# Reciprocal row sums inside the probability transposes: a diagonal in place of the identity, the sink as a score column, transposes two pairs behind the scores

## The reference

```python
# layer 0: the sink is one more logit, whose probability is dropped
p = jax.nn.softmax(jnp.concatenate([s_loc, s_ctx, sink_l], axis=-1), axis=-1)
o = (jnp.einsum('bhgnqk,bhnkd->bhgnqd', p[..., :nk].astype(v.dtype), vb)
     + jnp.einsum('bhgnql,bhld->bhgnqd', p[..., nk:nk + L].astype(v.dtype), vc))
...
# layer 1: no sink
p = jax.nn.softmax(jnp.concatenate([s_loc, s_ctx], axis=-1), axis=-1)
```

## Time and profile before

| | us |
|---|---|
| median of 3 runs | 1751.51 (1749.96 to 1753.03) |
| profiled execution, its own time | 1752.69 |
| its span in the trace | 1750.9 |
| TensorE busy | 1667.4 (95%) |
| VectorE, ScalarE, GpSimd busy | 708.4, 644.1, 676.9 |
| attention of layer 0 | about 269 to 358 |
| attention of layer 1, with the context values | about 1194 to 1315 |
| granted TensorE clock over the span | 0.99 |

### The profile page before, as it was taken

One profiled execution on the slowest core, in us unless ns is written; L12 is line 12 of the kernel. 1 busy time (PEld: TensorE's weight loads), 2 busy tenths in 40 slices (PEclk: granted clock), 3 DMA queues, 4 the chain that ended last, 5 costly groups with the idle time before them and its releaser, 6 DMA issues.

```text
span 1750.9 us, 25757 instructions
## 1 busy us (share of the span) xinstructions
PE 1667.4 (95%) x10178; PEld 1387.9 (79%) x10178; DVE 708.4 (40%) x1121; ACT 644.1 (37%) x1120; POOL 676.9 (39%) x456
## 2 busy tenths in 40 slices
PE   5999998999999999999899999999999899999997
PEld 2868886777877888878899878877887788888886
DVE  3335456717588735402555420005771551011103
ACT  4242215727422122213555343235772522222222
POOL 2212222038554544443542043334443444444443
PEclk9999999999999999999999999999999899999999
DMA  8643111023466746533556645433002353333331
GB/s 325 212 150 99 42 25 49 2 73 108 145 193 193 230 143 188 167 91 109 145 169 183 193 117 113 92 94 101 2 2 60 100 165 95 105 90 98 96 98 69
DMA packets 210131, 207.17 MB, mean 118 GB/s; under 512 B 16454, under 2 KB 180828, under 8 KB 209756
## 3 DMA queue, kind: packets, MB, share of 16 engines
q1 hardware_dynamic: 197352, 165.53, 31.7%
q10 hardware_dynamic: 12660, 39.99, 7.4%
HBM read 203.37 MB, written 2.13 MB: 117 GB/s over the span
## 4 chain that ended last, share of the span: by engine, by line
PE 82%; DVE 5%; issue 4%; POOL 3%; ACT 3%; DMA 2%; SPq 0%; ACTq 0%; POOLq 0%; DVEq 0%
PE ps L1689 39%; PE ps L1716 29%; PE ps L1867 3%; PE ps L1923 3%; PE ps L1888 3%; POOL w_lo L518 3%; DMA mod_early<-in_w_mod 1%; ACT w_hi L830 1%; PE ps L1763 1%; PE ps L1802 1%; DVE xs L1278 1%; PE ps L1935 1%; PE ps L2051 1%; DVE full L1227 1%; DMA w_raw<-in_w_ffn_in 1%
## 5 line engine op out<-in xcount | busy, mean ns | idle before, releaser
L518 POOL TENSOR_TENSOR w_lo<-w_raw,w_hi 128x1024 fp32r<-128x1024 f32 (+1 forms) x223 | 557.5, 2502 | 896.3 <-ACT w_hi L830 896.1
L1689 PE MATMUL ps<-h_hi,w_hi 128*128 128x512 f32 (+1 forms) x1488 | 496.7, 352 | 11.7 <-POOL w_lo L518 8.0
L1689 PE MATMUL ps<-h_hi,w_lo 128*128 128x512 f32 (+1 forms) x1488 | 492.0, 349 | 0.0
L1689 PE MATMUL ps<-h_lo,w_hi 128*128 128x512 f32 (+1 forms) x1488 | 491.0, 348 | 0.0
L830 ACT ACTIVATE w_hi<-w_raw 128x1024 fp32r<-128x1024 f32 (+1 forms) x275 | 287.2, 1046 | 354.2 <-PE ps L1716 342.8
L1689 PEld LDWEIGHTS ps<-h_hi,w_hi 128*128 128x128 f32 x1488 | 270.0, 189 | 56.6 <-issue 20.2
L1689 PEld LDWEIGHTS ps<-h_hi,w_lo 128*128 128x128 f32 x1488 | 269.8, 189 | 36.2
L1689 PEld LDWEIGHTS ps<-h_lo,w_hi 128*128 128x128 f32 x1488 | 269.8, 189 | 36.0
L518 DVE TENSOR_TENSOR w_lo<-w_raw,w_hi 128x1024 fp32r<-128x1024 f32 x52 | 69.2, 1332 | 200.5 <-ACT w_hi L830 197.5
L1716 PE MATMUL ps<-w_hi,hid_hi 128*128 128x512 f32 x440 | 136.7, 392 | 8.0 <-ACT mod_row L842 4.2
L1297 DVE TENSOR_TENSOR hid_f<-silu_g,ps 128x512 f32<-128x512 f32 (+1 forms) x66 | 39.3, 595 | 255.3 <-PE ps L1689 254.9
(11 more groups left out here) (213 smaller groups left out, 1790.4 us busy)
## 6 DMA issues: line engine op xcount, KB each, us to landing
w_raw<-in_w_ffn_in SPq DMA_DIRECT2D x132, 512.0 KB, 3.8
w_raw<-in_w_ffn_out SPq DMA_DIRECT2D x66, 512.0 KB, 3.5
mod_raw<-in_w_mod ACTq DMA_DIRECT2D x42, 512.0 KB, 4.5
w_raw<-in_na_w_in SPq DMA_DIRECT2D x32, 512.0 KB, 3.7
mod_early<-in_w_mod SPq DMA_DIRECT2D x30, 512.0 KB, 9.0
full<-in_w_mod ACTq DMA_DIRECT2D x15, 512.0 KB, 4.9
w_raw<-in_ab_w_in SPq DMA_DIRECT2D x9, 512.0 KB, 4.6
w_raw<-in_ab_w_in SPq DMA_DIRECT2D x16, 256.0 KB, 3.8
```

The lines of the kernel that those rows point to most:

```text
L518: eng.tensor_tensor(w_lo[:, u % RING, 0:width], w_raw[:, u % RAW, 0:width], w_hi[:, u % RING, 0:width].bitcast(F32), ALU.subtract).then_in ...
L1689: mm = pe.matmul(o[0], sta(x, o), mov(y, o), start=first and n == 0, stop=last and n == 2)
```

## The change

Every probability block is now multiplied by a diagonal matrix, where it was transposed by the identity: `pe.matmul` of the block against a 128x128 diagonal of the pair's reciprocal row sums. The transposed block comes out normalized. So the steps `shift`, `inverse`, `norms`, `inverse_rows` and `normalize` go, and `high` and `low` read the output's PSUM bank directly. The sink becomes column 0 of the score block in layer 0 (`prob0` has 1 + 5*128 columns), so that the row sum includes it. GpSimd writes that column (`sink_column`) and makes the two diagonals (`scale`): a power -1 of the two row sums, and a product of the identity with the result, 128x256, into one buffer, `full[:, 0:2]` in layer 0 and `scale1` in layer 1. `prob` has three buffers instead of two. Transposes stand two pairs behind the scores, values three. The third buffer of layer 1 lies where `gate_b` is, so ScalarE's load of the third gate rows moves behind attention of layer 1.

```diff
+            feed(sp("out0L") + 1)
+            def sink_column(p):
+                f = PAIRS[0][p][2]
+                if p >= 3:
+                    pool.wait_ge(at_p, 2 * (p - 2))
+                pool.tensor_scalar(prob0[:, p % 3, :, 0:1].rearrange("p x n -> p (x n)"), sink[:, f:f + 5:4], 1.0 / SCALE,
+                                   None, ALU.mult).then_inc(at_sink, 1)
+            def scale(layer, p):
+                q = PAIR0[layer] + p
+                n = CHUNK0[layer] + p // 2
+                pool.wait_ge(at_p, 2 * (q + 1))
+                if p:
+                    pool.wait_ge(at_ta, q)
+                    pool.wait_ge(at_tb, q)
+                    if fifths(layer, p - 1):
+                        pool.wait_ge(at_t5, fifths(layer, p - 1))
+                rows, inv = (x[:, 2 * (p % 2):2 * (p % 2) + 2] for x in (rowsum[:, n % 2, :], sm[:, n % 2, 3, :]))
+                pool.tensor_tensor(inv, rows, one_hot[:, 34:36], ALU.pow).then_inc(at_rinv, 1)
+                pool.wait_ge(at_rinv, q + 1)
+                one = ident[:]
+                one = bass.AP(one.tensor, one.offset, [list(one.ap[0]), [0, 2], [1, P]])
+                pool.tensor_tensor(scale_of(layer), one, bcast(inv, P), ALU.mult).then_inc(at_scale, 1)
+            for p in range(3):
+                sink_column(p)
+            for p in range(len(PAIRS[0])):
+                scale(0, p)
+                if p + 3 < len(PAIRS[0]):
+                    sink_column(p + 3)
             feed(sp("out0C"))
...
                     pool.wait_ge(v_mixed, p + 1)
+                if p:
+                    scale(1, p - 1)
+            scale(1, len(PAIRS[1]) - 1)
             feed(sp("out1L") + 7)
...
                 def softmax(p):
-                    n, c = s_cols(layer, p), c0 + p // 2
+                    n, c = s_cols(layer, p) + (layer == 0), c0 + p // 2
                     act.wait_ge(at_m, q0 + p + 1)
+                    if layer == 0:
+                        act.wait_ge(at_sink, p + 1)
...
-                for p in range(n_pairs + 3):
-                    if 1 <= p <= n_pairs:
-                        evacuate(p - 1)
-                    if p % 2 == 0 and p >= 4:
-                        inverse_rows(p // 2 - 2)
+                for p in range(n_pairs + 4):
+                    if p % 2 == 1 and p >= 5:
+                        high((p - 5) // 2)
+                    if 2 <= p <= n_pairs + 1:
+                        evacuate(p - 2)
                     if p < n_pairs:
                         softmax(p)
...
-                    if i == 6:
-                        gate_load(act, 2)
...
             attention(1, lambda: layer1_values("v1C", C_TILES))
+            act.wait_ge(at_p, 2 * (PAIR0[1] + len(PAIRS[1])))
+            act.wait_ge(at_ta, PAIR0[1] + len(PAIRS[1]))
+            act.wait_ge(at_tb, PAIR0[1] + len(PAIRS[1]))
+            gate_load(act, 2)
             feed(sp("out1L") + 7)
...
-                    if p >= 2:
-                        dve.wait_ge(at_ta, q0 + p - 1)
-                        dve.wait_ge(at_tb, q0 + p - 1)
+                    if p >= 3:
+                        dve.wait_ge(at_ta, q0 + p - 2)
+                        dve.wait_ge(at_tb, q0 + p - 2)
...
                 def turns(p):
                     n = s_cols(layer, p) // P
+                    pe.wait_ge(at_scale, q0 + p + 1)
                     for x in range(2):
-                        pe.wait_ge(at_p, 2 * (q0 + p) + x + 1)
                         claim(4 + x)
                         for j in range(min(n, 4)):
-                            mm = pe.transpose(ps(4 + x, j * P, (j + 1) * P), probs(p, x, j), ident[:])
+                            mm = pe.matmul(ps(4 + x, j * P, (j + 1) * P), probs(p, x, j), scale_of(layer)[:, x, :],
+                                           start=True, stop=True)
...
-                for p in range(n_pairs + 2):
+                for p in range(n_pairs + 3):
                     if p == 0:
                         start(lambda: scores(0))
                     elif p < n_pairs:
                         scores(p)
-                    if 1 <= p <= n_pairs:
-                        turns(p - 1)
-                    if p >= 2:
-                        values(p - 2)
-                        if p % 2 == 1:
-                            norms(p // 2 - 1)
+                    if 2 <= p <= n_pairs + 1:
+                        turns(p - 2)
+                    if p >= 3:
+                        values(p - 3)
```

More of the change, by code:

```diff
@@ L624, in scores_bank, with prob_of, scale_of @@
             return 2 * x if layer == 0 else 2 * x + p % 2
-        def mixed_out(layer):
-            return full[:, 0:2, :].rearrange("p k n -> p (k n)") if layer == 0 else on1[:]
+        def prob_of(layer, p, x):
+            if layer == 0:
+                return prob0[:, p % 3, x]
+            return prob1_c[:, x] if p % 3 == 2 else prob1[:, p % 3, x]
+        def scale_of(layer):
+            return full[:, 0:2, :] if layer == 0 else scale1[:]
         block = ctx.enter_context(nc.Block())
@@ L696, in _ @@
             pool.wait_ge(small_done, 3)
+            pool.memset(one_hot[:, 34:36], -1.0).then_inc(small_done, 1)
             pool.memset(one_hot[:, 1:2], 1.0).then_inc(small_done, 1)
+            pool.wait_ge(small_done, 5)
             fed = [0]
@@ L961, in attention @@
                         meanwhile()
-                    if p % 2 == 1 and p < n_pairs and layer == 0:
-                        c = c0 + p // 2
-                        act.wait_ge(at_shift, c + 1)
-                        act.activation(sm[:, c % 2, 1, :], sm[:, c % 2, 0, :], ACT.Exp).then_inc(at_sink, 1)
-                    if p % 2 == 0 and p >= 4:
-                        high(p // 2 - 2)
             act.dma_start(x_res[:, 0:LT, :], a["x"][0].rearrange("(t p) d -> p t d", p=P)).then_inc(x_in, 16)
@@ L1347, in evacuate @@
                     dve.tensor_copy(to[:, 1, 0:m], ps(5, 0, m)).then_inc(at_eb, 1)
[L1349 to L1375 removed]
                 def low(c):
                     t, g, f = pairs[2 * c]
[L1379 removed]
+                    src = ps(6 + (c0 + c) % 2, 0, 2 * P).rearrange("p (f n) -> p f n", f=2)
                     dve.wait_ge(at_hi, c0 + c + 1)
@@ L1394, in attention @@
                         maximum(p)
-                        if p % 2 == 1 and layer == 0:
-                            shift(p // 2)
-                    if p % 2 == 0 and 2 <= p <= n_pairs:
-                        inverse(p // 2 - 1)
-                    if 1 <= p <= n_pairs:
-                        evacuate(p - 1)
-                    if p % 2 == 0 and p >= 4 and p // 2 - 2 < n_pairs // 2:
-                        normalize(p // 2 - 2)
                     if p % 2 == 1 and p >= 5:
-                        low(p // 2 - 2)
+                        low((p - 5) // 2)
+                    if 2 <= p <= n_pairs + 1:
+                        evacuate(p - 2)
             dve.memset(c_pad[:], 0.0).then_inc(c_zero, 1)
@@ L1773, in modulation_sum @@
                 claim(bank)
-                pe.wait_ge(small_done, 4)
+                pe.wait_ge(small_done, 5)
                 pe.wait_ge(mod_acc, sums_done(KT * (b + 1) - 1))
@@ L1848, in attention @@
                 pairs, q0, c0 = PAIRS[layer], PAIR0[layer], CHUNK0[layer]
-                prob = (prob0, prob1)[layer]
                 def scores(p):
@@ L1894, in turns @@
                         for x in range(2):
-                            mm = pe.transpose(ps(4, x * P, (x + 1) * P), probs(p, x, 4), ident[:])
+                            mm = pe.matmul(ps(4, x * P, (x + 1) * P), probs(p, x, 4), scale_of(layer)[:, x, :],
+                                           start=True, stop=True)
                         mm.then_inc(at_t5, 1)
@@ L1927, in values @@
                                 mm.then_inc(at_o, 1)
-                def norms(c):
-                    bank = 6 + (c0 + c) % 2
-                    pe.wait_ge(at_rinv, c0 + c + 1)
-                    for i in range(2):
-                        for x in range(2):
-                            r = sm[:, (c0 + c) % 2, 3, 2 * i + x:2 * i + x + 1]
-                            mm = pe.matmul(ps(bank, (2 + i) * P, (3 + i) * P, 64 * x, 64 * x + 64),
-                                           bass.AP(r.tensor, r.offset, [list(r.ap[0]), [0, 64]]), ident[:],
-                                           start=True, stop=True, skip_group_check=True)
-                            mm.then_inc(at_rr, 1)
-                    read_by((bank,), (at_on, c0 + c + 1))
+                    if p % 2 == 1:
+                        read_by((bank,), (at_lo, c0 + p // 2 + 1))
                 n_pairs = len(pairs)
-                for p in range(n_pairs + 2):
+                for p in range(n_pairs + 3):
                     if p == 0:
```

63 lines of the change are left out of this document (16 added, 47 removed).

## The result

The changed kernel takes 1799.83 us (median of four runs; one of them was disturbed and is left out of the ratio, the other three lie between 1798.08 and 1800.41), the kernel before 1752.06 in the same comparison. The ratio is 1.0275 with an interval of 1.0258 to 1.0293: 2.75% slower. The forecast was 1793, with 1779 to 1812 as its range. The profiled execution took 1798.08 us, span 1795.7, against 1752.69 and 1750.9 before: +45.4, where the sum said +41.2.

What follows compares the result with a forecast made beforehand. TensorE's instruction stream plus its waits was taken as the bound. Terms 41.5 - 12.3 - 1.3 + 5.6 + 7.1 + 3.0 - 2.4 = +41.2 us, on 1752.69, gave a forecast of 1793 us, range 1779 to 1812.

Steps and rivals of the forecast that it cites:

- The bound: Whole kernel, especially both attention stretches: TensorE's instruction stream plus its waits sets the time; 82% of the chain.
- part F: Ends of both attention stages, before `out0L` and `out1L`: two of four steps go, -1.2 us each, -2.4 together.
- Part A: Attention in both layers: 432 transposes become float32 matmuls at 0.234 us instead of 0.129, +41.5 us.
- the rival built on the factor of four: Transposes of both layers: each matmul call costs 0.52 us, +169 us, total about 1920; chance 1%.
- the rival in which the matmul costs no more than the transpose: Transposes of both layers: calls under 0.166 us, kernel 1751 or 1736 us; chance 2% same, 2% faster.
- Part B: Attention chunks on TensorE: `norms` goes, 28 chunks at 0.54 less 0.10 us, -12.3 us.
- Part C: Two-block chunks of layer 0: the longer distance removes waits for the exponential, four of 0.35 us, -1.3 us.
- Part D: Two-block pairs and last pairs of each layer: `turns` waits for GpSimd's single diagonal buffer, +5.6 us.
- rival 1: Attention pairs: GpSimd becomes the pace, `scale` taking 2.4 us against a cover of 2.19; 1812 us, chance 17%.
- rival 2: Attention starts and diagonal latency cost nothing, falling from 15.7 to about 3 us; 1780 us, chance 15%.
- Part E: Starts of both attention stages: the first `turns` wait behind GpSimd's queue, +7.1 us in layer 0, +3.0 in layer 1.

Runs made afterwards that it cites:

- the run with both repairs: Changed kernel with GpSimd's sink columns ahead of `b_o` at layer 0's start and two diagonal buffers: 1786.21 us, ratio 1.0206 to the kernel before.
- the last experiment: SBUF-scaling kernel with plain transposes, VectorE's reciprocal and halved `b_o` in layer 0, but layer 1 as in the kernel before: 1745.68 us, ratio 0.9978 to the kernel before.

## Why the prediction was right, and where its sizes were off

**The bound.** Right. The kernel's time followed TensorE's stream: the two runs that change only the form of the calls move it by 42 to 44 us (by the ratios). VectorE and ScalarE were busy 15 and 12 us less, and what they lost can have shortened only the ends (part F).

**Part A, +41.5.** Right in mechanism, 3 to 7 us too small. The step that failed is the subtraction 1.87 - 1.03, for the two rows have different neighbours. The starts of the single records in the traces show it. Inside a group they are 0.112 us apart for the float32 matmuls, of L2051 and of L1885 alike, and 0.109 for the transposes; from the last record to the next group it is 0.203 to 0.205 in all three. But from the first record to the second it is 0.109 in L2051's group, which follows full-array matmuls, and 0.214 in L1885's, which follows scores. That 0.10 is the difference between 1.87 and 1.98, and the row of before lacks it, while the transposes had their smaller share (0.165 there, so 0.056 more) in the 1.03 already. So the price for a pair with four blocks is 1.98 - 1.03 = 0.95 and not 0.84, and a chunk of layer 1 takes 8.36 where 8.14 was said. With the measured groups the part is 40 x 0.95, plus 8 x (2.49 - 1.72) for five blocks (307.01 to 309.50 after) and 8 x (1.09 - 0.58) for two (359.85 to 360.94): 48.2 by the groups. In the run that has nothing else 44 of it showed. What the 0.10 is, the layout or the type of the neighbour, was not tested apart; behind values a group takes 1.98 as well (1341.53 to 1343.51 in the run with both repairs).

The Trainium skill (TensorE: Matmul & The Clock Gate, Terms) calls the transpose mode 4x faster for float32. Every run here has a factor of 2 for a 128x128 block, one record, 0.109 us behind the last, against two at 0.112, and the rival built on the factor of four is out. So is the rival in which the matmul costs no more than the transpose: it needed a call under 0.166 us, and a call takes 0.22.

**Part B, -12.3.** Right: 0.44 a chunk, by the 6.44 of the run with plain transposes. **Part C, -1.3**, has no row of its own after: the waits for the diagonal stand in its place. The run with the matmul form alone shows its size: layer 0 grew by 16.3 us there, 1.5 less than the 17.8 of its groups, as the longer calls cover those waits.

**Part D, +5.6.** Right: the run with two diagonals took 4.0 to 4.8 away. The power took 0.708 (0.70 taken, between 0.55 and 1.01) and the product 0.612 (0.68), by groups (count, busy us, mean ns, idle before):

```profile
L762 POOL TENSOR_TENSOR sm<-rowsum,one_hot 128x2 f32<-128x2 f32 x56 | 39.7, 708 | 91.7 <-PE ps L1885 59.5 <-PE ps L1893 25.6 <-ACT prob L972 6.5
...
L766 POOL TENSOR_TENSOR scale<-ident,sm 128x256 f32<-128x256 f32 x32 | 19.6, 612 | 2.5
```

The two-block waits were 0.47 (0.42 said), and the last pairs' 1.09 (1.06 said). In the middle of layer 1 there was one, of 0.46 (1250.33 above), so rival 1, GpSimd as the pace, did not come; and as the run that removes both the late start of layer 0 and the latency gains 10 us, rival 2, that they cost nothing, is out too.

**Part E, +7.1 and +3.0.** `turns(0)` came at 284.21 (283.5 said), and counted from the first scores it is 9.5 us later than before (8.2 said). Taking the other parts from layer 0's +23.1 (A 17.8, B -5.3, C -1.3, D 4.1, F -0.9) leaves 8.7 for this start, 1.6 more than said. The prediction left a term out here: ScalarE's table load of 1.28 us. In the kernel before it lay in an idle stretch, 3.92 us ahead of the first exponential:

```profile
269.27 1.28 ACT L930 ACT_TABLE_LOAD   x1 [0.40 <-ACT tri L884]
```

In the changed kernel it stands behind the wait for the sink column, between `b_o` and `turns(0)`, and the run that moves it out shortens that stretch by 1.34. The run that reorders GpSimd's queue shortened the stage by 6.6. At layer 1 `turns(1)` waited 3.44 us (3.5 said):

```profile
1230.45 3.78 PE L1885 MATMUL ps<-scale,prob 128*128 128x128 f32 x16 [3.44 <-POOL scale L766]
```

It stood behind the queue that the prediction lists, GpSimd's timeline:

```profile
1224.12 2.37 POOL L517 TENSOR_TENSOR w_lo<-w_raw,w_hi 128x1024 fp32r<-128x1024 f32 x1 [2.89 <-ACT w_hi L871]
1226.44 1.31 POOL L819 TENSOR_TENSOR bias_m<-rel,near_b 128x256 f32<-128x256 f32 x2
1227.88 1.03 POOL L830 COPY x_res<-c_v 64x1024 f32<-64x1024 f32 x1
1229.00 0.71 POOL L762 TENSOR_TENSOR sm<-rowsum,one_hot 128x2 f32<-128x2 f32 x1
1229.79 0.61 POOL L766 TENSOR_TENSOR scale<-ident,sm 128x256 f32<-128x256 f32 x1
```

TensorE was granted 0.50 over the next 4 us (1230.40 to 1234.40 above), its lower level of 1.2 GHz, and the group took its 3.78 us at that. By the same subtraction (26.1 - 30.4 + 7.0 - 1.2 - 0.5 + 0.9) the start of layer 1 cost 1.9 (3.0 said), so the two errors in E partly cancel.

**Part F, -2.4.** The idle before `out0L` and `out1L` fell from 2.24 and 2.28 to 1.35 and 1.37, so 0.9 each and not 1.2: -1.8.

**What had no place in the sum.** Behind `out1L` the changed kernel gained 2.6 us. In the profile of before TensorE ran the first groups there at a low clock, and after it did not; the windows of 5 us, before and then after:

```profile
1314.70:1319.70 5.00, 4.98 (x15) 3.95 (x16) 0.00 (x0) 0.00 (x0) 0.00 (x0) 0.66 0.00 0
```

```profile
1362.10:1367.10 5.00, 4.94 (x22) 4.12 (x23) 0.00 (x0) 0.00 (x0) 0.00 (x0) 1.00 0.27 102
```

Twelve records took 4.42 us before (1314.72 to 1319.14) and 2.82 after: 1.6 of the 2.6. The other 1.0 falls at 1374.6 to 1376.9 of before, where TensorE was again granted 0.50, and the changed kernel, at the same products (1420.4 to 1421.8), 0.98. The shorter idle looks like the cause of the first, but in the last experiment the idle before `out1L` was 2.28 again and the granted clock 1.00 behind it. From `out1L` to the end the kernel before takes 436.1 us, and the twelve other profiled executions, two of them with the old idle, 433.4 to 434.6. So that gain belongs to the one execution and is not shown to belong to the change. The -1.1 between the layers has the same root: a product of the feed-forward net between them ran at the lower level for 3.4 us before and at the full one after, which is worth 1.6; the windows, before and after:

```profile
752.30:755.70 3.40, 3.40 (x10) 2.66 (x9) 0.00 (x0) 0.00 (x0) 0.43 (x1) 0.50 0.54 148
...
774.30:777.70 3.40, 3.40 (x17) 2.79 (x16) 0.00 (x0) 0.00 (x0) 0.42 (x1) 1.00 0.50 154
```

With the measured sizes: A 48.2, B -12.3, C -1.3, D 5.8 (4.1 in layer 0, 1.2 at the end of layer 1 and the single 0.46), E 10.6, F -1.8, and the stretches outside -4.4, give the +44.8 of the spans; E is the remainder of the two stages, so only the other terms are tested by this. The prediction came within 4 us of the profiled execution (+45.4) and 7 of the median, and part of that is luck: A was 7 too small by its groups, while the 4.4 outside the stages, most of them the granted clock of the one execution of before, went the other way.

## What to carry to other kernels

A transpose through TensorE can take a diagonal instead of the identity and scale on the way, but it then is a real matmul and has to be priced as one. In float32 that doubled each call here, and where TensorE is the bound it outweighed all the work taken from engines that wait. Two cheaper forms were not tried: `pe.transpose` with the diagonal itself, and a product in fp32r, which the trace lists as one record for a call. When two rows are subtracted, see that they have the same neighbours in the stream, for the 0.1 us at the start of a group came back 56 times. A new step on a shared queue is dear at the starts and ends of a stage, where it meets what is already queued, and a new wait can carry a table load with it onto the path: check each stage's first and last pairs, and each layer by itself, since half of a change can pay (here layer 0, with cheap transposes and the scaling in place) where the whole does not.

## What the runs showed of the hardware

- GpSimd multiplies a tile by one scalar a row at 1.57 us for 512 columns, 0.93 for 256 and 1.89 for 640, but rounds 512 columns in 0.61 us. Its power takes 0.71 us for two columns a row, between the 0.55 for one and the 1.01 for four.
- In the run that scales in SBUF, VectorE's instructions grew beside GpSimd's. VectorE's timeline, then GpSimd's:

```profile
1251.34 2.25 DVE L1383 TENSOR_SCALAR negm<-raw_max 128x2 f32<-128x2 f32 x1
1251.42 2.17 DVE L1393 COPY prob_t<-ps 128x512 f32<-128x512 f32 x1
```

```profile
1250.44 1.57 POOL L753 TENSOR_SCALAR prob_c<-prob_c,sm 128x512 f32<-128x512 f32 x1
1251.97 1.60 POOL L829 TENSOR_TENSOR bias_m<-rel,near_b 128x192 f32<-128x192 f32 x4
```

  Both VectorE instructions end at 1253.59, as GpSimd's second one does (1253.57); the copy takes 0.69 us in the changed kernel. The Trainium skill (SBUF — State Buffer, Who interferes with whom) describes an exclusive lock of a shared port pair for a whole instruction. The common end agrees with it; whether the copy out of PSUM was held itself, or only stood behind the small instruction in VectorE's queue, no run here shows.
- ScalarE's table load is placed at the first exponential that needs it and behind that instruction's wait, so that a wait put ahead of the exponential puts 1.28 us behind itself. The Trainium skill (ScalarE: Activation LUTs, What ACT_TABLE_LOAD costs) gives 1283 ns for the load, and the trace has 1283; the drain that it adds, 1380 ns, shows in no row here, where the exponential starts 0.01 us behind the load (279.85 + 1.28 to 281.14).
- Low clock after a wait isn't a fixed price: 2.28 us of idle ahead of `out1L` was followed by 0.66 over 5 us in one execution and by 1.00 in another.
